# Attention blocks of two neighbouring heads issued together, on alternate halves of the TensorE array

## The reference, cut to what matters

```python
# context tokens: softmax over the 128 context keys; latent tokens: 256 latent keys and 128 cached keys
s = jnp.einsum('bqkgd,bskd->bkgqs', qblk, k)          # scores, contraction over 64
p = jax.nn.softmax(s, axis=-1)
return jnp.einsum('bkgqs,bskd->bqkgd', p, v)          # values
...
out_s = merge_heads(oa, ob, attn_w_out[e])            # the 16 heads' outputs times a 1024 x 1024 weight
```

## Time and profile before

| | us |
|---|---|
| median of 3 runs (1719.39 to 1721.28) | 1719.74 |
| span of the profiled execution | 1717.1 |
| PE busy / weight loads busy | 1660.1 / 1589.1 |
| DVE / ACT / POOL busy | 1067.5 / 578.3 / 81.3 |
| attention stage: first transposes to the output product | 447.7 to 548.3 |
| of it the main loop | 463.0 to 548.3 |

### The profile page before, as it was taken

How to read it: one execution, slowest core, us unless ns; L and a number is a source line. 1 busy time by engine, 2 the same in 40 slices (tenths; PEclk the granted TensorE clock), 3 DMA queues, 4 the chain that set the end, 5 groups by cost and what they waited for, 6 DMA issues and landing times.

```text
span 1717.1 us, 25878 instructions
## 1 busy us (share of the span) xinstructions
PE 1660.1 (97%) x9927; PEld 1589.1 (93%) x9927; DVE 1067.5 (62%) x1803; ACT 578.3 (34%) x751; POOL 81.3 (5%) x48
## 2 busy tenths in 40 slices
PE   8899999988899899999989999998999998999998
PEld 4899999988756899999989999998999998999998
DVE  3677668767754766767966777697745435334323
ACT  2423232253344442322234333222642325333222
POOL 1200000034100100000010000001000001000000
PEclk9999999989999899999989999999999998999999
DMA  9755547526200445555634545564533332433332
GB/s 310 187 182 164 192 159 244 170 85 207 77 1 31 157 146 173 177 189 196 224 120 135 193 161 195 190 226 157 186 124 96 125 123 85 136 122 122 124 130 77
DMA packets 222917, 261.81 MB, mean 152 GB/s; under 512 B 14502, under 2 KB 207494, under 8 KB 222854
## 3 DMA queue, kind: packets, MB, share of 16 engines
q1 hardware_dynamic: 222854, 260.95, 46.3%
HBM read 258.64 MB, written 2.29 MB: 152 GB/s over the span
## 4 chain that ended last, share of the span: by engine, by line
PE 86%; issue 6%; DVE 4%; ACT 1%; POOL 1%; DMA 0%; POOLq 0%; SPq 0%; ACTq 0%; DVEq 0%
PE ps L1066 15%; PE ps L1067 15%; PE ps L1069 15%; PE ps L1022 9%; PE ps L1024 9%; PE ps L1023 9%; PE ps L1055 3%; PE ps L1037 2%; PE ps L1257 1%; DVE macc L754 1%; PE ps L1126 1%; PE ps L1294 1%; POOL hrs L503 1%; PE ps L1363 1%; DVE w_lo L731 1%
## 5 line engine op out<-in xcount | busy, mean ns | idle before, releaser
L731 DVE TENSOR_TENSOR w_lo<-raw,w_hi 128x2048 fp32r<-128x2048 f32 x164 | 380.0, 2317 | 282.3 <-ACT w_hi L527 282.2
L1066 PE MATMUL ps<-x_hi,w_hi 128*128 128x384 f32 x1536 | 523.3, 341 | 13.2 <-ACT x_hi L553 9.9
L1067 PE MATMUL ps<-x_hi,w_lo 128*128 128x384 f32 x1536 | 520.1, 339 | 0.0
L1069 PE MATMUL ps<-x_lo,w_hi 128*128 128x384 f32 x1536 | 517.1, 338 | 0.0
L527 ACT ACTIVATE w_hi<-raw 128x2048 fp32r<-128x2048 f32 x169 | 322.9, 1911 | 344.2 <-PE ps L1024 326.3
L754 DVE SCALAR_TENSOR_TENSOR macc<-mraw,cT,macc 128x256 f32<-128x256 f32 x896 | 359.9, 478 | 0.0
L1066 PEld LDWEIGHTS ps<-x_hi,w_hi 128*128 128x128 f32 x1536 | 292.1, 190 | 17.0 <-issue 13.3
L1067 PEld LDWEIGHTS ps<-x_hi,w_lo 128*128 128x128 f32 x1536 | 292.1, 190 | 0.0
L1069 PEld LDWEIGHTS ps<-x_lo,w_hi 128*128 128x128 f32 x1536 | 291.3, 190 | 0.0
L1022 PE MATMUL ps<-act_hi,w_hi 128*128 (+1 forms) x832 | 281.8, 339 | 0.0
L1024 PE MATMUL ps<-act_hi,w_lo 128*128 (+1 forms) x832 | 279.6, 336 | 0.0
(11 more groups left out here) (154 smaller groups left out, 1310.7 us busy)
## 6 DMA issues: line engine op xcount, KB each, us to landing
raw<-ffn_w_gu SPq DMA_DIRECT2D x88, 1024.0 KB, 5.1
mraw<-mod_w SPq DMA_DIRECT2D x66, 1024.0 KB, 7.4
raw<-ffn_w_down SPq DMA_DIRECT2D x44, 1024.0 KB, 4.8
raw<-sgu_w_in SPq DMA_DIRECT2D x16, 1024.0 KB, 5.5
raw<-attn_w_in SPq DMA_DIRECT2D x9, 1024.0 KB, 5.0
raw<-sgu_w_out SPq DMA_DIRECT2D x8, 1024.0 KB, 4.8
mfirst<-mod_w SPq DMA_DIRECT2D x6, 1024.0 KB, 12.8
raw<-attn_w_out SPq DMA_DIRECT2D x4, 1024.0 KB, 4.9
```

The source lines that it names most:

```text
L731: nc.vector.tensor_tensor(w_lo[q0 % 2][:, :], raw[q0 % 2][:, :], w_hi[q0 % 2][:, :].bitcast(F32), ALU.subtract).then_inc(lo_done, 1)
L1066: mm(out, hi[:, cols], x_hi[:, k, :], start=(k == 0), stop=False)
L1067: mm(out, lo[:, cols], x_hi[:, k, :], start=False, stop=False)
L1069: last = mm(out, hi[:, cols], x_lo[:, k, :], start=False, stop=(k == KD - 1))
```

## The change

Blocks are renumbered so that two neighbouring heads (a pair) go together: six blocks to a pair, in the order kind 0 of the even head, kind 0 of the odd head, kind 1 of both, kind 2 of both. PE issues the score matmuls of two blocks one after the other; the even head lies in rows 0 to 63, the odd head in rows 64 to 127. For that the GQA heads are laid out so that head parity again gives the half, and the GQA keys get a second copy with the halves exchanged (two DVE copies of 64 partitions, from PSUM). The value products of the two heads alternate, product by product, between columns 0 to 63 and 64 to 127. Scores now use four PSUM banks and transposed probabilities two; the groups of queries and keys rotate through four banks; blocks 0 to 3 go ahead of the loop where 0 to 2 did.

```diff
-            kT_g = sb("kT_g", [P, T + P], scope=s)
+            kT_g = sb("kT_g", [P, 2, T + P], scope=s)
...
+        def head_of(b):
+
+            pair, r = divmod(b, 6)
+            return 2 * pair + r % 2, r // 2
+
+        def pT_of(hh):
+
+            if (hh // 2) % 2 == 0:
+                return pT_lat[:, hh % 2, :, :]
+            return tmp[:, 2 * (hh % 2):2 * (hh % 2) + 2, :].rearrange("p a t -> p (a t)").rearrange("p (k q) -> p k q", k=3)
...
         # ACT
-            for b in range(3):
+            for b in range(4):
                 softmax(b)
             put_qk([g for g in range(5, 13) if g not in TR_DVE])
...
+            for j in range(2, 24 + 4):
+                for b in (2 * j, 2 * j + 1):
+                    if b < 48:
+                        softmax(b)
+                for b in (2 * j - 4, 2 * j - 3):
+                    if b < 48:
+                        put_pT(b)
+                if j >= 6 and j % 3 == 0:
+                    o_hi(j // 3 - 2)
...
         # DVE
+            dve.wait_ge(tr_act, 11)
+            for half in range(2):
+                src = ps[HD * half:HD * half + HD, TR_BANK[12 % 4], 0:T + P]
+                nc.vector.tensor_copy(kT_g[HD - HD * half:P - HD * half, 1, :], src).then_inc(tr_dve, 1)
+            for j in range(2, 24 + 4):
+                for b in (2 * j, 2 * j + 1):
+                    if b < 48:
+                        top(b)
+                for b in (2 * j - 2, 2 * j - 1):
+                    if b < 48:
+                        normalise(b)
...
         # PE
+            def scores(j):
+
+                for b in (2 * j, 2 * j + 1):
+                    hh, kind, qT, kT = score_operands(b)
+                    if b >= 4:
+                        pe.wait_ge(exp_done, b - 3)
+                    if kind == 0:
+                        mm(ps[:, b % 4, 0:P], qT[:, 0:P], kT[:, 0:P], start=True, stop=True).then_inc(s_pe, 1)
+                    else:
+                        na = hh < NH
+                        last = mm(ps[:, b % 4, 0:T], qT[:, P * kind:P * kind + P], kT[:, P:P + T], start=True, stop=not na)
+                        if not na:
+                            last.then_inc(s_pe, 1)
+                for b in (2 * j, 2 * j + 1):
+                    hh, kind = head_of(b)
+                    if hh < NH and kind:
+                        mm(ps[:, b % 4, 0:NLAT], perm[:, :], bias[:, kind - 1, hh, :], start=False, stop=True).then_inc(s_pe, 1)
...
-                bank = TR_BANK[g % 5]
+                bank = TR_BANK[g % 4]
...
-                if g >= 5:
-                    pe.wait_ge(tr_act, g - 4)
+                if g >= 4:
+                    pe.wait_ge(tr_act, g - 3)
...
             pe.wait_ge(tr_act, 11)
-            pe.wait_ge(tr_dve, 2)
+            pe.wait_ge(tr_dve, 4)
...
             def p_transposes(b):
                 pe.wait_ge(prob_done, b + 1)
-                if b >= 3:
-                    pe.wait_ge(pT_done, b - 2)
+                if b >= 2:
+                    pe.wait_ge(pT_done, b - 1)
...
+            def values(pair):
+
+                pe.wait_ge(pT_done, 6 * pair + 6)
...
+                for k in range(4):
+                    for hh in (2 * pair, 2 * pair + 1):
+                        half = hh % 2
+                        out = ps[HD * half:HD * half + HD, 6 + pair % 2, :]
...
+                            last = mm(out[:, P:T], vk, pT_of(hh)[:, k - 1, :], start=(k == 1), stop=(k == 3))
+                last.then_inc(o_pe, 1)
+
+            for j in range(2, 24 + 3):
+                if j < 24:
+                    scores(j)
+                for b in (2 * j - 4, 2 * j - 3):
+                    if b < 48:
+                        p_transposes(b)
+                if j >= 5 and j % 3 == 2:
+                    values(j // 3 - 1)
...
-TR_BANK = (5, 3, 6, 7, 4)
+TR_BANK = (5, 4, 6, 7)
```

More of the change, by code:

```diff
@@ L645, in put_pT @@
                         .then_inc(pT_done, 1)
             def o_hi(pair):
-                act.wait_ge(o_pe, 2 * pair + 2)
+                act.wait_ge(o_pe, pair + 1)
                 nc.scalar.activation(x_hi[:, pair, :], ps[:, 6 + pair % 2, 0:T], ACT.Copy).then_inc(oh_done, 1)
-            for b in range(3):
+            for b in range(4):
                 softmax(b)
             put_qk([g for g in range(5, 13) if g not in TR_DVE])
[L654 to L659, removed]
@@ L953, in _ @@
                 dve.wait_ge(tr_pe, g + 1)
[L954 to L960, removed]
+                nc.vector.tensor_copy(dst, ps[:, TR_BANK[g % 4], 0:n]).then_inc(tr_dve, 1)
+            dve.wait_ge(tr_act, 11)
[9 more added lines that the diff above has]
+                        normalise(b)
+                if j >= 7 and j % 3 == 1:
+                    o_lo(j // 3 - 2)
             o_lo(7)
@@ L1242, in _, with score_operands @@
                       + [(qk_g, n, None) for n in range(4)] + [(qk_g, 4, kc_g[:, :])])
-            def scores(b):
-                hh, kind = divmod(b, 3)
+            def score_operands(b):
+                hh, kind = head_of(b)
+                rows = slice(HD * (hh % 2), HD * (hh % 2) + HD)
                 if hh < NH:
[L1246 to L1250, removed]
-                if b >= 3:
[L1252 to L1260, removed]
@@ L1271, in _ @@
                     pe.wait_ge(bias_done, 2)
-                    for b in range(3):
-                        scores(b)
-                    mod_psum(MOD_M + MOD_IN - 1, 0, 4, 4 * (MOD_IN - 1), True)
+                    scores(0)
+                    scores(1)
+                    mod_psum(MOD_M + MOD_IN - 1, 0, 5, SPARE + 4 * (MOD_IN - 1), True)
                     pe.wait_ge(mod_done, outs_until(MOD_M + MOD_IN))
@@ L1295, in p_transposes @@
                 last.then_inc(pT_pe, 1)
[L1297 to L1301, removed]
+            def values(pair):
+                pe.wait_ge(pT_done, 6 * pair + 6)
+                if pair >= 2:
                     pe.wait_ge(ol_done, pair - 1)
[L1303 to L1320, removed]
+                for k in range(4):
+                    for hh in (2 * pair, 2 * pair + 1):
+                        half = hh % 2
+                        out = ps[HD * half:HD * half + HD, 6 + pair % 2, :]
+                        if hh < NH:
+                            v, cache, cols = v_na, vc_na, slice(HD * hh, HD * hh + HD)
+                        else:
+                            kv = (hh - NH) // 4
+                            v, cache, cols = vg_, vc_g, slice(HD * kv, HD * kv + HD)
+                        if k == 0:
+                            mm(out[:, 0:P], v[:, 0, cols], pT_ctx[:, hh % 4, :], start=True, stop=True)
+                        else:
+                            vk = v[:, k, cols] if k < 3 else cache[:, cols]
+                            last = mm(out[:, P:T], vk, pT_of(hh)[:, k - 1, :], start=(k == 1), stop=(k == 3))
```

43 lines of the change are left out of this document (22 added, 21 removed).

## The result

The changed kernel takes 1696.11 us (median of four runs, 1693.88 to 1698.93) against 1719.57 for the kernel before (four runs, 1717.19 to 1721.28): a ratio of 0.986, interval 0.985 to 0.987.

What follows compares the result with a forecast made beforehand. PE was taken to bound the attention stage. 1717.1 - 9.8 (mode changes) + 1.5 (two banks) + 2.0 (start) - 9.7 (halves side by side) = 1701.1; with 2.6 around it, 1703.7 us, range 1698.0 to 1714.0.

Steps and rivals of the forecast that it cites:

- DVE and ACT still fit: Loop: DVE and ACT work, 5.2 to 5.9 us a pair, fits in the 7.8 us of a GQA pair.
- Mode changes: Attention heads: a pair has as many array mode changes as one head had; net -9.8 us.
- Two banks: PE's transposes wait for ACT's copy of block b - 2: 0.6 us in GQA pairs, 0.9 at first step; +1.5.
- The start: Ahead of the loop: fourth softmax +0.35, four group banks +0.27, second GQA key copy 1.3; +2.0 us.
- the prediction's last rival: Ahead of the loop: longer waiting could lower the clock, 1 to 2 us; inside the range, no chance of its own.
- Halves side by side: Scores and values: passes on different halves overlap, loads one pass ahead; scores 3.2, values 7.4, extra waits +0.9; -9.7 us.
- free end: Scores and values: passes on different halves run freely beside each other; -14.2 us instead of -9.7.
- Loads run ahead: Scores and values: both loads of the second half are done before its turn; 1699.2 us, chance 0.15.
- Columns alone and rows alone: Only one kind of half overlaps: columns (values) 1706.0 us, chance 0.08; rows (scores) 1711.1 us, chance 0.10.
- No overlap: Scores and values: float32 passes on two halves don't overlap, but changing half costs nothing; 1713.4 us, chance 0.18.
- a shown load for each change of half: Scores and values: each change of half shows its weight load, 5.5 us; 1718.9 us, no change, chance 0.09.
- emptying at each change: Scores and values: each change of half empties the array, 13.2 us; 1726.6 us, slower, chance 0.09.

Runs made afterwards that it cites:

- Without overlap: The changed kernel with the odd head's scores and values on the even head's half: 1718.20 us; with PE's key-copy wait moved behind the first scores too: 1713.60 us.
- the copies in front: The changed kernel with ACT copying transposed probabilities of two blocks out of PSUM ahead of its step's two exponentials instead of behind them: 1690.56 us, ratio 0.983.
- the late wait: The changed kernel with PE's wait for the second key copy moved from ahead of the loop to behind the first scores: 1694.05 us, ratio 0.984.
- the third bank: The changed kernel with three PSUM banks for transposed probabilities and one for outputs, instead of two and two: 1693.23 us, ratio 0.984.
- the second key copy alone: The kernel before with only the unused second GQA key copy and PE's wait for it ahead of the loop added: 1722.67 us, ratio 1.0013.

## Why the prediction was right in direction and too small in size

**What bounds the kernel: right.** PE's pieces were the time, and what was taken from them came off the end. That "DVE and ACT still fit" was wrong for the GQA pairs. The sum of their work fits (5.6 and 5.5 us in a pair that PE could do in 5.96); the order of ACT's list didn't. The prediction compared work with time and not the chain of one step. It had named the sign itself: ACT and DVE pieces in the chain of the middle pairs, and about 4 us of the GQA pair's chain are such.

**Mode changes: right.** 1.30 a head were forecast for NA and 1.20 for GQA, less 0.16 of waiting. Without overlap an NA pair went from 11.85 to 10.58, which is 1.27, and a GQA pair from 9.93 to 9.11, which is 0.82 instead of 1.04. With the two banks, forecast -9.8 + 1.5 = -8.3 in the loop, measured -7.5.

**Two banks: the place right, the size wrong once overlap works.** Without overlap GQA pairs lose 0.2 against the forecast, little. With it the GQA pair is 7.05, 1.09 above what the copies in front reach: 4.4 us over the four pairs, where 0.16 a pair and another 0.9 for the faster PE stood in the sum. At the first step PE waits 0.82 us (1.11 where the clock is up), where 0.9 was forecast.

**The start: +2.0 forecast, +3.2 measured.** Term by term, from the two timelines: the fourth softmax costs 0.34 (0.35 forecast). From the first key copy on ACT to the last, 2.22 us became 3.21, +0.99 (0.27 forecast). In the six runs with the same four banks whose low clock ended at most 0.3 us behind the start of the first key copy, it is 2.61 to 2.62, and the fifteen transposes take 2.54 to 2.55: so the four banks cost 0.39, and the other 0.60 is the low clock, at which the fifteen took 3.14 and ACT waited for PE. The second key copy is 1.41 on DVE and 1.5 on the way (1.3 forecast, bounds 1.0 to 1.4). Another 0.3 lies ahead of the modulation. Then the clock fell again in the first step, 3.4 us at half speed, 1.7 lost. That was the prediction's last rival, 1 to 2 us, and it shows at about that size: the loop of the run with the late wait, where the clock is up, is 1.3 shorter. Where the clock stays up with the early wait, the start costs 2.6 instead of 3.2 (values in turns of two: 16.09 against 13.53).

**Around the sum.** The 2.6 us that the forecast puts around the program are 1.8 where one execution has both a time and a span (1697.49 against 1695.7). The low end of the range, from the terms that it names, comes to 1699.2 - 0.3 = 1698.9 and not to 1698.0; the measured time is below either.

**Halves side by side: the step that failed, -9.7 forecast, -18.9 to -19.3 measured.** The step took over from the earlier trace rows that passes start strictly in their order, each after the one ahead has started and its load is done. So A2, waiting for its half, held back B1, on the other half. The timeline shows the opposite: B1 starts 6 ns after A1, past A2, which starts 0.2 later. The two values orders show that about three waiting passes are passed over. Scores: 0.21 forecast for a pair of 384 columns, 1.49 - 0.84 = 0.65 measured, and 0.64 - 0.42 = 0.22 where nothing was forecast for 128 columns. Values: 0.92 forecast a pair, 3.17 - 1.66 = 1.51 measured. For an NA pair that makes 2 x 0.65 + 0.22 + 1.51 = 3.03, against the 2.91 between 10.58 and 7.66; a GQA pair yields only 2.06, since ACT's order takes the rest. The "free end", -14.2 (its terms as written, 8 x (0.75 + 1.27) - 1.4, come to -14.8), was no end: it kept the passes in order too, and so the range that was built from it was too high. Rows of a trace in which no two neighbours lie on different halves can't bound what two halves do; the bound that needs no such rule is half of all streaming on halves. That is 8 x 3.0 / 2 = 12 us for values and 8 x (2 x 1.28 + 0.43) / 2 = 12 for scores, 24 with nothing lost to other engines.

**The rivals.** Loads run ahead (1699.2) named the right mechanism in part, and is nearest: loads do go in twos and starts are a few ns apart, but it left the passes in order. The Trainium skill ("TensorE: Matmul & The Clock Gate", Part 3) gives for a pack of tiles the time of one matmul and about 4 ns for each further one; the score pair, 0.84 for two heads as for one, with starts 6 to 7 ns apart, agrees, for float32 too. The same part lets loads overlap only on other rows; the value products' loads, on the same rows, go in twos beside running passes, and it also has all matmuls in order, which the timeline of values head after head contradicts. Columns alone and rows alone (1706.0 and 1711.1) are out by the runs with one kind of half. No overlap, a shown load for each change of half, and emptying at each change (1713.4, 1718.9, 1726.6) are out: values in turns of one product take 1.66 and in turns of two 1.71, so a change of half costs nothing that shows. The Trainium skill ("TensorEngine Tiling (Array Packing)", Key Properties) has it so: only a change of mode drains the engine.

**What stays open.** What lets the clock fall or stay up after the pause. Nine profiled executions have the early wait and its pause of about 2.2 us: in six of them the clock falls within 2.3 us of the loop's start, for 3.4 us (the change, values head after head, the third bank), 10.2 (both heads on one half, scores on one half) or 13.7 (the second key copy alone); in three it stays up through the loop. In the four without that pause, the kernel before and the three with the late wait, it stays up as well. So the pause goes with the fall, but doesn't decide it alone, and no run was made to tell what does. The number three for the passes that are passed over rests on two orders; it could be a limit in something else that comes to three passes here.

## What to carry to other kernels

Where neighbouring float32 matmuls use half of the array's rows or columns, put them in turns on the two halves: here the second head's scores and values came free, and even turns of two products do. Afterwards ask of each other engine's list in one step, not of its busy share, what the faster engine will wait for; turning one list around was worth another 5 us here. And keep a wait that only later work needs away from the head of a loop: here that let the loop start 1.0 to 1.4 us earlier, though the times of the two runs with the late wait can't be told from those without it.

## What the runs showed of the hardware

- Two float32 matmuls on different halves of rows, or of columns, run at once, 6 to 7 ns apart, each at its own full pace: 0.84 us for two heads' scores as for one, 1.66 for two heads' values instead of 3.17.
- A matmul that waits for its half doesn't hold up one behind it for the other half; about three passes can be passed over: with a head's eight passes issued ahead of the other's, the other starts beside the fifth, and the group takes 2.36 us, against 1.66 in turns and 3.17 on one half.
- After a pause of about 2.2 us in which PE waits, the array ran at 1.2 GHz for 3.4 to 13.7 us though it was busy nearly throughout, in six of nine profiled executions: 1.7 to 6 us lost.
